# Last output rows and the final norm taken in two halves of the tokens, with their weights streamed twice and the stores in eight pieces of two tiles

## The reference

```python
def rms_norm(x, g): ...      # x * rsqrt(mean(x * x, over the features) + EPS) * g

y = jnp.concatenate([y_conv, y_att], axis=-1)      # 512 + 512 features
h = h + y @ w_out[l]                               # 1024 -> 1024
return rms_norm(h, final_g)
```

## Time and profile before

| | |
|---|---|
| median of 3 runs | 3517.61 us (3515.96 to 3518.24) |
| profiled execution, its own time | 3518.09 us |
| span of the profiled execution, first to last instruction | 3516.3 us |
| PE busy | 3384.4 us, 96% of the span |
| POOL busy | 1220.3 us, 35% |
| DVE busy | 1766.4 us, 50% |
| mean granted TensorE clock | 0.989 |

### The profile page before, as it was taken

One profiled execution on the slowest core, in us unless ns is written; L12 is line 12 of the kernel. 1 busy time (PEld: TensorE's weight loads), 2 busy tenths in 40 slices (PEclk: granted clock), 3 DMA queues, 4 the chain that ended last, 5 costly groups with the idle time before them and its releaser, 6 DMA issues.

```text
span 3516.3 us, 40431 instructions
## 1 busy us (share of the span) xinstructions
PE 3384.4 (96%) x16204; PEld 2702.8 (77%) x16204; DVE 1766.4 (50%) x2045; ACT 757.1 (22%) x1140; POOL 1220.3 (35%) x534
## 2 busy tenths in 40 slices
PE   7999999999999999989999999999999999999997
PEld 6777877778888888867886668888888876767775
DVE  5344544463333333488765653223223357988835
ACT  4233100030000000242224440000000023144352
POOL 2212334434444444332331133333434432432322
PEclk9999999999999999999999999999999999999998
DMA  2101211111111111121211111111111110111111
GB/s 98 46 31 45 90 48 48 48 36 48 48 48 48 50 51 48 36 68 54 84 47 34 35 36 48 48 48 48 48 48 48 48 36 31 53 41 41 41 36 66
DMA packets 47294, 171.80 MB, mean 49 GB/s; under 512 B 5472, under 2 KB 6112, under 8 KB 47200
## 3 DMA queue, kind: packets, MB, share of 16 engines
q1 hardware_dynamic: 38016, 138.43, 12.0%
q10 hardware_dynamic: 9184, 32.03, 2.6%
HBM read 165.71 MB, written 4.72 MB: 48 GB/s over the span
## 4 chain that ended last, share of the span: by engine, by line
PE 86%; DVE 7%; issue 3%; ACT 3%; POOL 1%; DMA 0%; ACTq 0%; DVEq 0%; POOLq 0%
PE acc L396 70%; PE acc L414 4%; PE acc L838 2%; PE acc L814 2%; PE acc L433 1%; DVE conv_slots L1986 1%; PE acc L483 1%; PE acc L791 1%; PE acc L803 1%; DVE rstd L701 1%; POOL w_lo L2300 0%; DVE h L998 0%; PE acc L537 0%; DVE band_scores L906 0%; POOL w_hi L2286 0%
## 5 line engine op out<-in xcount | busy, mean ns | idle before, releaser
L2286 POOL TENSOR_TENSOR w_hi<-raw,zero 128x1024 fp32r<-128x1024 f32 x264 | 517.4, 1960 | 2240.0 <-PE acc L396 1600.2
L396 PE MATMUL acc<-x_hi,w_hi 128*128 128x512 f32 x2512 | 778.7, 391 | 8.0 <-POOL w_lo L2300 2.3
L396 PE MATMUL acc<-x_hi,w_lo 128*128 128x512 f32 x2512 | 774.8, 390 | 0.0
L396 PE MATMUL acc<-x_lo,w_hi 128*128 128x512 f32 x2512 | 774.6, 390 | 0.0
L2300 POOL TENSOR_TENSOR w_lo<-raw,w_hi 128x1024 fp32r<-128x1024 f32 x262 | 696.5, 2658 | 20.5
L998 DVE TENSOR_TENSOR h<-h,acc 128x1024 f32<-128x1024 f32 x320 | 390.3, 1221 | 386.5 <-PE acc L396 384.6
L396 PEld LDWEIGHTS acc<-x_hi,w_hi 128*128 128x128 f32 x2512 | 470.6, 188 | 109.0 <-issue 9.1
L396 PEld LDWEIGHTS acc<-x_lo,w_hi 128*128 128x128 f32 x2512 | 472.4, 188 | 98.7
L396 PEld LDWEIGHTS acc<-x_hi,w_lo 128*128 128x128 f32 x2512 | 472.3, 188 | 98.4
L493 ACT ACTIVATE hid_hi<-hid 128x1024 fp32r<-128x1024 f32 x44 | 46.7, 1061 | 925.7 <-DVE hid L1386 469.7
L1986 DVE SCALAR_TENSOR_TENSOR conv_slots<-conv_slots,par 128x1024 f32<-128x1024 f32 x120 | 227.5, 1896 | 4.1
(11 more groups left out here) (358 smaller groups left out, 3997.4 us busy)
## 6 DMA issues: line engine op xcount, KB each, us to landing
raw<-blocks SPq DMA_DIRECT2D x264, 512.0 KB, 3.3
h<-x_t ACTq DMA_DIRECT2D x8, 512.0 KB, 8.4
h<-x_t ACTq DMA_DIRECT2D x1, 4096.0 KB, 14.0
q_past<-q_dram ACTq DMA_DIRECT2D x8, 512.0 KB, 5.6
w_own<-r_dram ACTq DMA_DIRECT2D x8, 512.0 KB, 6.8
out_t<-out_rows ACTq DMA_DIRECT2D x8, 512.0 KB, 3.0
near_bias<-bias ACTq DMA_DIRECT2D x4, 896.0 KB, 4.6
band_bias<-bias ACTq DMA_DIRECT2D x4, 640.0 KB, 4.0
```

The costliest lines, as they stand in the source:

```text
L396: ins = pe.matmul(acc[s][:, c], w[:, slot, tile, :], part[:, c], start=(n == 0 and m == 0), stop=(n == last and m == 2))
L2286: pool.tensor_tensor(hi, whole, nothing, ALU.add).then_inc(hi_split, 1)
```

## The change

The four blocks of `row_block` and the final norm are replaced by `end_tensor`, `end_scalar` and `end_vector`. They make the first 512 tokens of all output tiles, then the other 512. The stream holds the four weight blocks twice. A block now serves 24 matmuls instead of 48: two output tiles (`o`) of one half of the tokens, side by side in one accumulator. DVE adds a pair of tiles at once (128x2x512), ACT squares the pair into its own slot of `raw_squares`, and DVE adds up the pairs in `normed` (L2156) and then the two halves of that into 512 columns of `rstd` (L2160). The mean of the first half (L2105) stands on PE behind the first block of the second half. The rows of the first half (L2167, 128x512) stand on DVE between the second and the third addition of the second half, and their stores, four of two half tiles each, between two squares on ACT.

```diff
             near_rows(pe, t)
             await_parts(pe, t, CONV_TILES)
-            row_block(pe, t, [(g_hi[:, k, :], g_lo[:, k, :]) for k in range(CONV_TILES)])
...
+        def end_tensor(pe, t):
+            def rows(half):
+                c = token_half(half)
+                for b in range(KT // 2):
+                    slot, s = take_block(pe, t), claim(pe, t)
+                    for o in range(2):
+                        for k in range(CONV_TILES):
+                            for m, (w, part) in enumerate(((w_hi, g_hi), (w_hi, g_lo), (w_lo, g_hi))):
+                                ins = pe.matmul(acc[s][:, token_half(o)], w[:, slot, o * CONV_TILES + k, :],
+                                                part[:, k, c], start=(k == 0 and m == 0),
+                                                stop=(k == CONV_TILES - 1 and m == 2))
+                                if o == 0 and k == 0 and m == 0:
+                                    ins.then_inc(w_used, 1)
+                    ins.then_inc(acc_full[s], 1)
+                    take_turn(pe, t)
+                    if half and b == 0:
+                        mean(0)
...
+            rows(0)
+            rows(1)
+            keep_clock(pe, 14)
+            mean(1)
+
+        def end_scalar(act, t, ch):
...
+            for b in range(KT // 2):
+                square_pair(0, b)
+            square_pair(1, 0)
+            root(0)
+            square_pair(1, 1)
+            store(0)
+            square_pair(1, 2)
+            square_pair(1, 3)
+            root(1)
+            store(1)
+
+        def end_vector(dve, t, ch):
...
+            for half in range(2):
+                add_pair(half, 0)
+                add_pair(half, 1)
+                sum_pair(half, 1)
+                if half:
+                    rows(0)
+                add_pair(half, 2)
+                sum_pair(half, 2)
+                add_pair(half, 3)
+                sum_pair(half, 3)
+            rows(1)
...
-            norm_tensor(pe, t, (14, 0))
+            end_tensor(pe, t)
...
-            norm_scalar(act, t, ch, "out", rows=True)
+            end_scalar(act, t, ch)
...
-            norm_vector(dve, t, ch, "out", "final_g", rows=True)
+            end_vector(dve, t, ch)
...
     yield from row_blocks(w_out, 4 + HEAD_PAIRS - 1)
-    yield from row_blocks(w_out, 0, 4)
+    for _ in range(2):
+        yield from row_blocks(w_out, 0, 4)
```

More of the change, by code:

```diff
@@ L2077, in conv_tensor, with token_half, mean @@
             await_parts(pe, t, CONV_TILES)
-            row_block(pe, t, [(g_hi[:, k, :], g_lo[:, k, :]) for k in range(CONV_TILES)])
+        END_MEAN = acc_all[:, 3 * TOK:4 * TOK]
+        def token_half(half):
+            return slice(half * HALF, (half + 1) * HALF)
+        def end_tensor(pe, t):
[15 more added lines that the diff above has]
+                        mean(0)
+            def mean(half):
+                pe.wait_ge(sum_ready, t.next("sum_ready"))
+                c = token_half(half)
+                pe.matmul(END_MEAN[:, c], mean_w[:, :], rstd[:, c], start=True, stop=True).then_inc(mean_full, 1)
+            rows(0)
+            rows(1)
+            keep_clock(pe, 14)
+            mean(1)
@@ new lines, in end_scalar, with square_pair, root, store @@
+        def end_scalar(act, t, ch):
+            def square_pair(half, b):
+                s = t.turn % 2
+                pass_acc(t)
+                act.wait_ge(acc_free[s], t.count(f"acc{s}"))
+                act.activation(raw_squares[:, half * 4 + b, :].rearrange("p (o n) -> p o n", o=2),
+                               h[:, 2 * b:2 * b + 2, token_half(half)], ACT.Square).then_inc(squared, 1)
+            def root(half):
+                c = token_half(half)
+                act.wait_ge(mean_full, t.next("mean_full"))
+                inverse_root(act, ch, rstd[:, c], END_MEAN[:, c], "eps6").then_inc(root_ready, 1)
+            def store(half):
+                c = token_half(half)
+                for b in range(KT // 2):
+                    act.wait_ge(rows_ready, t.next("rows_ready"))
+                    act.dma_start(out_t[2 * b * P:2 * (b + 1) * P, c].rearrange("(k p) n -> p k n", p=P),
+                                  out_rows[:, 2 * b:2 * b + 2, c]).then_inc(stored, 16)
+            for b in range(KT // 2):
+                square_pair(0, b)
[7 more added lines that the diff above has]
+            store(1)
@@ new lines, in end_vector, with add_pair, sum_pair, rows @@
+        def end_vector(dve, t, ch):
+            partial = normed[:, 0, :]
+            def add_pair(half, b):
+                s, c = await_acc(dve, t), token_half(half)
+                dve.tensor_tensor(h[:, 2 * b:2 * b + 2, c], h[:, 2 * b:2 * b + 2, c],
+                                  acc[s].rearrange("p (o n) -> p o n", o=2), ALU.add).then_inc(acc_free[s], 1)
+            def sum_pair(half, b):
+                if b == 1:
+                    t.next("squared")
+                dve.wait_ge(squared, t.next("squared"))
+                ch.sync()
+                ch.link(dve.tensor_tensor(partial, raw_squares[:, half * 4, :] if b == 1 else partial,
+                                          raw_squares[:, half * 4 + b, :], ALU.add))
+                if b == KT // 2 - 1:
+                    ch.sync()
+                    dve.tensor_tensor(rstd[:, token_half(half)], partial[:, token_half(0)], partial[:, token_half(1)],
+                                      ALU.add).then_inc(sum_ready, 1)
+            def rows(half):
+                c = token_half(half)
+                dve.wait_ge(root_ready, t.next("root_ready"))
+                for k in range(KT):
+                    ins = dve.scalar_tensor_tensor(out=out_rows[:, k, c], in0=h[:, k, c], scalar=col("final_g", k),
+                                                   in1=rstd[:, c], op0=ALU.mult, op1=ALU.mult)
+                    if k % 2:
+                        ins.then_inc(rows_ready, 1)
+                    else:
+                        ch.link(ins)
+                    if k % 2:
+                        ch.sync()
+            for half in range(2):
[9 more added lines that the diff above has]
+            rows(1)
```

## The result

| | before | changed |
|---|---|---|
| median of 13 runs each | 3516.31 us | 3522.70 us |
| span of the profiled execution | 3516.3 us | 3520.9 us |
| from the start of the first addition behind the change to the end of the span | 60.8 us | 65.7 us |

The ratio of the times is 1.0015, with a 95% interval of 1.0008 to 1.0022: slower by 2.8 to 7.7 us. The ratio lies inside the 0.2% (7.0 us) that the prediction called about what a measurement can tell from no change, but the interval is clear of 1, so 13 runs of each kernel do tell them apart. The forecast was 3522.9.

What follows compares the result with a forecast made beforehand. PE bounds the kernel (busy 96%), then a 22.7 us serial tail. The shorter tail saves about 5 us, but DVE comes 6.2 later and serial work and the slow mean consume the saving: +5.3, 3522.9 us; range 3515.5 to 3526.0.

Steps and rivals of the forecast that it cites:

- main case: The whole end of the kernel: the split makes it 5.3 us slower, median 3522.9 us; chance 0.6.
- PE and the second weight stream: Row products: blocks last 5.45 us, POOL's split is done with 0.5 us to spare, so streaming costs PE nothing.
- The sums held by `w_lo`: DVE's sums of pairs wait for POOL's `w_lo`, ending 5.93 us after block start T instead of 3.9; margin 0.2.
- PE's wait at the first mean: Behind block 4, PE idles 1.2 us for the first half's sum; the mean then takes 0.8.
- The eight tiles in front of ready additions: First half's tiles on DVE take 5.4 plus about 3.9 us held by POOL's padding block split, until 3499.8.
- The series of two additions, squares and sums: Behind the first eight tiles, additions of pairs 2 and 3 with squares and sums take 7.9 us, to 3507.7.
- The slow mean: Last mean on PE after 9 us idle, at 1.2 GHz: 2.1 us instead of 1.15 at full clock.
- The last tiles: Second half's eight output tiles on DVE begin at 3512.5 us and take 5.4, to 3517.9.
- The last store: From DVE's last tile to the end of the span: 3.7 us, as before, ending at 3521.6.
- The ports matter little: Rival: sums and tiles not held by POOL; end at 3517.0 or 3515.8, full gain 3511.7; chance 0.2.
- TensorE at 1.2 GHz after the wait at the first mean: Rival: PE's clock falls after that wait, shifting blocks 5 to 7 by 1.7 or 3.4 us: 3524.6 to 3526.3; chance 0.2.
- POOL bounding PE: Rival: sums win against `w_lo`, costing 0.4 us on up to four blocks; 3521 to 3523, inside the forecast.

Runs made afterwards that it cites:

- the five experiments that keep this stretch as it is: Edits of the changed kernel not differing from it up to the second half's pair 1 addition, which comes 29.53 to 29.55 us after the first addition.
- the mean one block later: Changed kernel with the first half's mean one block later on PE and, on ACT, the square of pair 1 ahead of the root; stretch 64.0 us, one run.
- the PSUM run: Changed kernel with the running sum of squares and the inverse root kept in PSUM; stretch 58.2 us, ratio to before 0.9993.
- the idle matmuls: Changed kernel with 44 idle matmuls instead of 14 in front of the last mean; stretch 64.8 us, ratio to before 1.0012.
- the last kernel: Changed kernel with sums and root in PSUM, no padding block, first half's stores by SP, its tiles spread over DVE's gaps; stretch 56.0 us, ratio to before 0.9987.

## Why the prediction was right

Its main case came to be, by its own steps. Measured times are put 0.35 later here, where they are compared with the forecast's, since all of the changed kernel's stretch began 0.35 earlier than that of the kernel before.

- **PE and the second weight stream.** Blocks of 5.45 with POOL done half a microsecond ahead: right; in the trace PE doesn't wait for `w_split` once. The stream costs PE no wait for a block. What it costs is on DVE: POOL's splits hold the sums and the tiles, and the padding block is one of them.
- **The sums held by `w_lo`.** Forecast: they end at T+5.93, that of pair 1 of the second half at 3490.5. They took 3.09 to 3.47 in place of 1.22, and that one ended at 3490.55 (3490.9 on the forecast's scale, of which 0.3 are the later block of the next point). The race against `w_lo`, which I had given a margin of 0.2, was decided by 0.01 at its narrowest (3487.07 against 3487.08), and the same way in the changed kernel and the five experiments that keep this stretch as it is; with so little between them that is in part luck. With the mean one block later, the sum of pair 1 came first, and the `w_lo` behind it took 3.25. That the lock is what holds them is shown by the PSUM run.
- **PE's wait at the first mean.** Forecast 1.2, measured 1.20. Block 5 came 0.3 later than forecast, because the mean in front of it took 1.12 on PE where 0.8 had been put: the addition of pair 1 began at 3484.74 (3485.1 on the scale of the forecast, which had 3484.8).
- **The eight tiles in front of ready additions.** Forecast 9.3, measured 9.19, of which 3.8 are the padding block's.
- **The series of two additions, squares and sums.** 7.9 forecast; from 3499.59 to 3507.34 are 7.75.
- **The slow mean.** 2.1 forecast; the chain gives 2.09. The clock is its cause (0.95 of it came back with the idle matmuls).
- **The last tiles.** Forecast to begin at 3512.5; at 3512.18, 3512.5 on the same scale. 5.4 each way.
- **The last store.** This term was 0.35 too large: 3.7 were taken over from before, and 3520.9 - 3517.57 = 3.35 were there. It is the whole difference between the +5.3 forecast and the +4.9 measured.

That the median of 3522.70 lies so close to the 3522.9 is in part luck. The forecast stood on a median of 3517.6 for the kernel before; with 13 runs it is 3516.31, and the two medians are 6.4 apart where 5.3 was forecast. The ratio of 1.0015 is worth 5.3, the stretch 4.9.

The rivals. The ports matter little: wrong, they were worth 7.5. TensorE at 1.2 GHz after the wait at the first mean: it stayed at PEclk 1.00 with a wait of 1.20. POOL bounding PE: not once in the changed kernel.

Where the gain went is now in numbers. The tail was indeed shortened, but the order put 9.2 us of DVE work that nobody waited for ahead of 7.75 us that everything waited for. Undoing that one thing alone brings the stretch from 65.7 to 59.2, below the 60.8 of before; the ports alone bring it to 58.2. The two overlap, since both take away the same lateness of DVE: alone they are worth 6.5 and 7.5, and the last kernel, with both and without the padding block, gained 9.7.

## What to carry to other kernels

When a tail is split so that its first half can hide beside the second, the hidden half must stand in the gaps of its engine and never ahead of what feeds the critical chain: list, for that engine, what is ready when, and put the work nobody waits for behind it. If two engines share a resource by whole instructions, count what the other one does in the new place of each moved instruction, work that is useless too; moving one operand elsewhere (here to PSUM) can end the dispute without changing the order. The value of such a fix holds only as long as that engine is late: 3.8 us and 0.2 us for the same edit here.

## What the runs showed of the hardware that was not expected

- DVE tiles of 512 columns with two SBUF operands ran at 0.67 each without POOL. In the changed kernel POOL and DVE took turns, one instruction each: the first two of the eight tiles took 2.42 and 2.88 and ended 0.55 after `w_hi` and `w_lo`, and the `w_lo` between them grew from 2.40 to 2.72. That is the 3.8 us; the other six tiles were not held.
- ACT wrote a square of 128x1024 to PSUM in 1.03 and to SBUF in 1.06; Ln and Exp of 512 columns took 0.66 and 0.58 where the root stays in PSUM, 0.69 and 0.63 where it is written to SBUF (and, for Exp, read from there).
- A store of 512 KB with rows of 2 KB took no longer to land than one with rows of 4 KB: the page of the changed kernel has a median of 2.9 us, that of before 3.0.
- The unchanged 3450 us in front varied by 6.5 us between profiled executions of these kernels (first addition at 3450.97 to 3457.52), as much as the order on DVE was worth. The time goes with the mean granted clock of the run: in the 56 runs of the kernel before that stand beside the experiments it averages 3511.1 at a clock of 0.992 (4 runs) and 3518.8 at 0.988 (16 runs). Why the clock differs from run to run is open.
